# Convolution rows of a two-block layer: statistics copied among the gated tiles, bias and gates loaded in another order, the last row normed in halves

## The reference, cut to what matters

```python
u = h @ w_in + b_in
a, ga, z = split(u, 3)
glu = a * sigmoid(ga)
c = depthwise_conv(glu, w_dw, taps=31) + b_dw
c = silu(layer_norm(c, norm_g, norm_b))
y = (c * silu(z)) @ w_out + b_out
h = layer_norm(DN_ALPHA * h + y, post_ln_g, post_ln_b)   # for each token
```

## Time and profile before

| | |
|---|---|
| runs | 2434.09, 2439.77, 2440.2 us; median 2439.77 |
| profiled execution | 2432.7 us, of it span 2431.0 us |
| PE busy | 2330.9 us, 96% of the span |
| DVE, ACT, POOL busy | 1388.2, 1125.8, 878.7 us |
| convolution's rows | about 535 us to 771 us of the span |

### The profile page before, as it was taken

The page is one execution under the profiler, slowest core; times in us unless marked ns, Lnnn a source line. Parts: engine busy times, 40 slices in busy tenths (PEclk is TensorE's granted clock), DMA queues, the critical chain, the costliest instruction groups (busy, mean ns, idle before and its releaser), DMA issues. The chain is left out here.

```text
span 2431.0 us, 34611 instructions
## 1 busy us (share of the span) xinstructions
PE 2330.9 (96%) x13338; PEld 1214.8 (50%) x13338; DVE 1388.2 (57%) x2330; ACT 1125.8 (46%) x2179; POOL 878.7 (36%) x673
## 2 busy tenths in 40 slices
PE   8999999997997999999999998998899998999998
PEld 4555555543444455555555554444545554444443
DVE  6999999974654234334334334677267776235422
ACT  7766666576653234334344334333155665233311
POOL 3988888877882110101101010443033333000000
PEclk9999999998998999999999999999999999999999
DMA  5011111143333000101000003223410000101322
GB/s 203 29 55 44 37 39 39 47 141 100 126 121 148 1 1 12 46 1 49 1 5 10 1 1 130 79 92 108 64 43 10 19 1 1 40 18 55 110 101 90
DMA packets 52218, 134.67 MB, mean 55 GB/s; under 512 B 5391, under 2 KB 23439, under 8 KB 51032
## 3 DMA queue, kind: packets, MB, share of 16 engines
q1 hardware_dynamic: 52056, 132.46, 16.3%
HBM read 96.65 MB, written 35.80 MB: 54 GB/s over the span
## 5 line engine op out<-in xcount | busy, mean ns | idle before, releaser
L1146 DVE SCALAR_TENSOR_TENSOR cv_tap_sum<-cv_glu,cv_prm,cv_tap_sum 128x1024 f32<-128x1024 f32 x326 | 418.9, 1288 | 11.9 <-ACT cv_tap_sum L648 2.4
L902 POOL TENSOR_TENSOR mixed<-mixed,cv_tap_products 128x1024 f32<-128x1024 f32 x153 | 364.2, 2381 | 77.5 <-ACT cv_tap_products L663 62.1
L91 PE MATMUL cv_proj<-H_hi,cv_w_ga 128*128 128x416 f16 (+1 forms) x640 | 217.0, 339 | 7.9 <-DVE H_lo L1119 7.9
L92 PE MATMUL cv_proj<-H_lo,cv_w_ga 128*128 128x416 f16 (+1 forms) x640 | 217.0, 339 | 0.0
L93 PE MATMUL cv_proj<-H_hi,cv_w_ga 128*128 128x416 f16 (+1 forms) x640 | 217.0, 339 | 0.0
L91 PE MATMUL gm_vr<-gm_wvr_hi,H_hi 128*128 128x512 f16 (+1 forms) x544 | 202.8, 373 | 0.0
L92 PE MATMUL gm_vr<-gm_wvr_lo,H_hi 128*128 128x512 f16 (+1 forms) x544 | 202.8, 373 | 0.0
L93 PE MATMUL gm_vr<-gm_wvr_hi,H_lo 128*128 128x512 f16 (+1 forms) x544 | 202.8, 373 | 0.0
L1769 POOL TENSOR_TENSOR gm_q_inter<-gm_q_rel,gm_block_decays 128x512 f32<-128x512 f32 x16 | 16.8, 1048 | 467.0 <-ACT gm_block_decays L1846 467.0
L663 ACT ACTIVATE cv_tap_products<-cv_glu,cv_prm 128x1024 f32<-128x1024 f32 x138 | 151.8, 1140 | 35.9 <-POOL mixed L902 35.8
L2125 DVE SCALAR_TENSOR_TENSOR gm_v_r<-gm_vr,gm_v_r 128x256 f32<-128x256 f32 x64 | 27.2, 425 | 236.9 <-ACT gm_v_r L1865 236.9
(11 more groups left out here) (443 smaller groups left out, 5751.8 us busy)
## 6 DMA issues: line engine op xcount, KB each, us to landing
cv_w_stage<-conv_w SPq DMA_DIRECT2D x24, 512.0 KB, 3.9
mixed<-gla_w SPq DMA_DIRECT2D x8, 1024.0 KB, 6.7
go_rows<-h_rows SPq DMA_DIRECT2D x16, 512.0 KB, 3.9
h_rows<-go_rows SPq DMA_DIRECT2D x16, 512.0 KB, 2.8
pl_sums_a<-h_rows SPq DMA_DIRECT2D x16, 512.0 KB, 3.5
out<-pl_sums_a SPq DMA_DIRECT2D x16, 512.0 KB, 2.6
cv_tap_products<-gate_z SPq DMA_DIRECT2D x24, 256.0 KB, 3.9
mixed<-xT SPq DMA_DIRECT2D x12, 416.0 KB, 8.0
```

Source lines behind the costliest of these rows:

```text
L91: nc.tensor.matmul(out, w_hi, x_hi, start=first, stop=False)
L92: nc.tensor.matmul(out, w_hi, x_lo, start=False, stop=False)
L902: nc.gpsimd.tensor_tensor(c_unit(U), c_unit(U), prod[:, r % 3, :], ALU.add).then_inc(s_add, 1)
L1146: nc.vector.scalar_tensor_tensor(out=acc_unit(U), in0=window(U, k), scalar=col(U // 2, k), in1=acc_unit(U), op0=ALU.mult, op1=ALU.add).the ...
```

## The change

1. ACT copies the sums of group 2 between the gated tiles 5 and 6 of group 1, before it norms row 0; they were copied after it, at row 1. The tiles themselves keep their order.
2. For groups 3 and 4 (rows 3 and 7), ACT copies the sums before the row's root and norming; it did so after them.
3. SP loads the bias and row 1 before the wait for the last convolution product, and the first gates of group 1 after it; five of these gates now stand ahead of the two layer-norm vectors, three did before. ACT scales the bias before gated tiles 0 and 1 of group 1, and POOL adds it to row 0 before them.
4. The last row is normed by ACT in two halves; DVE copies the low half of row 14 before it multiplies and adds the vectors of the last row, no longer after; and the last row's transposes go to two PSUM banks of its own (those of the means and spreads), so that they wait for no copies of row 15, only for the group statistics to be used up (`c_n`).

```diff
+        last_pt = [acc[:, 512 * h:512 * h + 512] for h in range(2)]
+        def turned(s, h):
+            return (last_pt if s == LAST else pt)[h]
...
                 for b in range(2):
                     sp.wait_ge(s_szo[b], 16 * KT * NTT // 2)
-                sp.wait_ge(s_add, slot(UNITS - 1, n_products(UNITS - 1)) + 1)
-                for k in range(R):
-                    load_gate(1, k)
                 sp.wait_ge(o_lo, KT)
                 vector(bias_bc, bias_dram, s_bv)
                 load_row(1)
+                sp.wait_ge(s_add, slot(UNITS - 1, n_products(UNITS - 1)) + 1)
+                for k in range(R + 2):
+                    load_gate(1, k)
                 sp.wait_ge(c_m, KT)
                 vector(g_bc, g_dram, s_vec)
                 vector(b_bc, b_dram, s_vec)
                 for s in range(NS + 1):
                     if s == 0:
-                        for k in range(R, KT):
+                        for k in range(R + 2, KT):
                             load_gate(1, k)
...
                 squares(2, range(CG))
-                gated(1, range(2))
                 act.wait_ge(s_bv, 16)
                 nc.scalar.activation(bias_bc, bias_bc, ACT.Copy, scale=1.0 / ALPHA).then_inc(s_bias, 1)
+                gated(1, range(2))
                 squares(2, range(CG, KT))
+                gated(1, range(2, 6))
+                copy_sums(2)
+                gated(1, range(6, KT))
                 for s in range(NS + 2):
-                    gated(*UNITS_AT.get(s, (0, ())))
-                    if (s, 0) in SUMS:
-                        copy_sums(SUMS[s, 0])
+                    if s:
+                        gated(*UNITS_AT.get(s, (0, ())))
...
+                    if (s, 1) in SUMS:
+                        copy_sums(SUMS[s, 1])
                     if s < NS:
...
-                        nc.scalar.activation(tile(s), tile(s), ACT.Identity, scale=sd[0:n, b, 1:2],
-                                             bias=sd[0:n, b, 2:3]).then_inc(s_u, 1)
-                    if (s, 1) in SUMS:
-                        copy_sums(SUMS[s, 1])
+                        for h in range(2) if s == LAST else (slice(0, 2),):
+                            x = tile(s).rearrange("p (a n) -> p a n", a=2)[:, h]
+                            mm = nc.scalar.activation(x, x, ACT.Identity, scale=sd[0:n, b, 1:2], bias=sd[0:n, b, 2:3])
+                            mm.then_inc(s_u, 1)
...
+                add_bias(0)
                 gated(1, range(2))
-                add_bias(0)
...
-                        if s:
+                        if s == LAST:
+                            pe.wait_ge(c_n, len(GROUPS) * KT)
+                        elif s:
                             pe.wait_ge(s_th, 2 * s + h - 1)
                             pe.wait_ge(s_tl, 2 * s + h - 1)
```

More of the change, by code:

```diff
@@ L874, in _ @@
                             nc.scalar.activation(H_hi[:, 4 * h:4 * h + 4, at:at + n],
-                                                 pt[h].rearrange("p (k n) -> p k n", k=4)[:, :, 0:n], ACT.Copy).then_inc(s_th, 1)
+                                                 turned(s - 2, h).rearrange("p (k n) -> p k n", k=4)[:, :, 0:n],
+                                                 ACT.Copy).then_inc(s_th, 1)
+                    if (s, 1) in SUMS:
+                        copy_sums(SUMS[s, 1])
                     if s < NS:
@@ L1043, in transposes @@
                             c = (4 * h + q) * P
-                            mm = nc.tensor.transpose(pt[h][:, q * P:q * P + n], tile(s)[:, c:c + P], ident[0:n, 0:n])
+                            mm = nc.tensor.transpose(turned(s, h)[:, q * P:q * P + n], tile(s)[:, c:c + P], ident[0:n, 0:n])
                         mm.then_inc(s_tr, 1)
@@ L1277, in _ @@
                                                 ALU.mult).then_inc(s_nm, 1)
[L1278 to L1285, removed]
                     if s >= 2:
@@ L1290, in _ @@
                             nc.vector.tensor_tensor(H_lo[:, 4 * h:4 * h + 4, at:at + n],
-                                                    pt[h].rearrange("p (k n) -> p k n", k=4)[:, :, 0:n],
+                                                    turned(s - 2, h).rearrange("p (k n) -> p k n", k=4)[:, :, 0:n],
                                                     H_hi[:, 4 * h:4 * h + 4, at:at + n], ALU.subtract).then_inc(s_tl, 1)
+                    if s == LAST:
+                        for h in range(2):
+                            c = slice(h * 512, h * 512 + 512)
+                            dve.wait_ge(s_vec, 16 * 2)
+                            dve.wait_ge(s_u, NS + h)
+                            nc.vector.tensor_tensor(tile(LAST)[:, c], tile(LAST)[:, c], g_bc[:, c], ALU.mult).then_inc(s_lg, 1)
+                            dve.wait_ge(s_lg, h + 1)
+                            nc.vector.tensor_tensor(tile(LAST)[:, c], tile(LAST)[:, c], b_bc[:, c], ALU.add).then_inc(s_lh, 1)
 def gla_out(nc, ahead, next_loads, rows_in, vecs, rows_out, pre_g, gs, M, H_hi, H_lo):
```

## The result

The changed kernel took 2423.26 us in the median of 4 runs, the kernel before 2439.58 us: a ratio of 0.9941, 95% interval 0.9922 to 0.9959. That is 14 us by the ratio (16.3 between the medians) where 8.55 us were forecast. Timed again with 12 runs against 20 of the kernel before, the ratio was 0.9969 (0.9956 to 0.9982), 7.6 us of 2435.6. The profiled executions lie 9.1 us apart, 2432.7 and 2423.57 us.

A forecast was written before the change was run, and what follows sets the result against it. The prediction took POOL, ACT and DVE, releasing one another, to bound the kernel until row 13. It summed 4.2 us there and 4.35 us at the last row to 8.55 us, forecasting 2431.2 us from 2439.77, range 2425 to 2437.

The forecast's parts named there:

- The bound: Until row 13: POOL, ACT and DVE waiting on one another set the pace; PE's earlier gains are waited away there.
- the ring: POOL, ACT and DVE releasing one another tile after tile until row 13; its start, mean_square(2), moves 4.2 us sooner.
- PE's waits: Rival for the rows: PE's waits of 7.4, 2.8 and 0.4 us bound and return; 19 us in all, chance 0.07.
- Copies of group 2: Before row 0's norming: earlier copies let mean_square(2) start at 556.2 us instead of 560.42, gaining 4.2 us.
- POOL's stall: At gate 6 of group 1: POOL waits for a silu issued behind the copies, 1.35 us (bounds 0 and 2.2).
- PE's new idle before row 2: Before row 2: PE waits anew for the low parts of group 1, some 2.5 us.
- Bias and gates: At group 1's first tiles: bias lands 4.25 us after issue, gates in time, and tile 3's 1.11 us gate wait goes.
- The start: Mean_square(2), with earlier copies, bias and gates: everything until row 13 comes 4.2 us sooner.
- Later copies: Groups 3 and 4, copied before the rows' norming: PE's 2.78 and 0.37 us waits go, worth 0.
- The last row: At the end: last DVE instruction and barrier come 4.35 us sooner, bounds 3.5 and 4.9.
- slow behind its gap: Row 15's transposes: PE taken at the 1.2 GHz level after its idle, 1.94 us for eight.
- Sum: Whole kernel: 4.2 us until row 13 plus 4.35 us at the end, 8.55 us.

The follow-up runs named there:

- late_copies_only: Kernel before with only the copies of groups 3 and 4 moved ahead of the rows' norming; ratio 1.0011 (1.0001 to 1.0022).
- start_only: Kernel before with group 2's copies among the gated tiles and the new bias and gate order, no later copies or end; ratio 0.9984 (0.9974 to 0.9994).
- silu_first: Changed kernel with the silu of group 1's tile 6 issued before tile 5's high part and group 2's copies; ratio to the kernel before 0.9968.
- copies2_only: Kernel before with only group 2's copies moved among the gated tiles; row 13 at 175.63 us behind the memset, no ratio given.
- after_again: The changed kernel timed and traced once more, no further edit; ratio to the kernel before 0.9969 (0.9956 to 0.9982).
- after: The changed kernel's first trace, against the kernel before; profiled execution 2423.57 us.
- before_again: The kernel before timed and traced once more as a control, no edit; ratio 1.0004 (0.9993 to 1.0014).
- end_only: Kernel before with only the change's edits of the last row; ratio 0.9989 (0.9977 to 1.0).
- best: Changed kernel with the silu of tile 6 issued earlier, but bias and gate loads and bias order as before; ratio 0.9958 (0.9943 to 0.9974).
- bias_only: Kernel before with only the new order of bias and gates, no moved copies; row 13 at 178.82 us behind the memset, no ratio given.

## Why the prediction came out as it did

**The bound.** Right: the ring of POOL, ACT and DVE sets when row 13 starts, and taking PE's own waits away gains nothing. late_copies_only shows it from one side, start_only from the other (2.8 to 4.1 us where PE's waits promised 7 and more).

**Copies of group 2.** The mechanism and its terms hold: mean_square(2) foreseen at 556.2, measured at 556.43 in an execution 0.4 us late; POOL's stall 1.35 foreseen, 1.33 measured; PE's new idle before row 2 some 2.5 foreseen, 3.17 measured. silu_first shows that the stall was a cost of this order and not of the copies.

**Bias and gates.** The landing was 4.1 us after the issue (4.25 taken), and no gate held the first tiles. The 3.2 us that the prediction works out from the Trainium skill's page "DMA: Bandwidth & Descriptors" are too short for it; the page gives that fit for transfers issued by GpSimd, and these are SyncE's. But I compared with one trace, in which a late gate cost 1.11 us at tile 3; only that trace and copies2_only (0.67 us) show such a wait among the eight with the old loads (with the new ones after_again alone waits, 0.23 us at a later tile). Wrong was to let the early bias count as a gain of the ring. With the old loads ACT and POOL gate tiles 0 and 1 while the bias is on its way; with the new ones they do it after the bias, which takes POOL 3.7 us, and the 4 us of earlier landing only pay for that. With the old loads the ring's start follows the landing: in the five traces without a late gate the square stands 21.8 us behind it (7.64 and 29.46, 9.46 and 31.24). Behind three gates the bias took 6.2 to 8.0 us from its issue in the eight traces, ahead of them 4.1 to 4.5 us in the five with the new loads. So the new loads seem mostly to narrow the spread, row 13 at 175.2 to 175.6 in three traces where the six with old loads and old copies spread over 1.8 us. The start is worth 3.6 us against the mean of the old ones; 4.2 was mis-sized by the late gate.

**Later copies.** 0, as foreseen, and for the reason foreseen (late_copies_only).

**The last row.** 4.35 foreseen, 4.15 measured. That PE was taken to be slow behind its gap was wrong in part: the gap of 2.81 us was not always followed by the slow level. Eight transposes took 1.23 us in `after`, 1.94 in silu_first.

**Sum.** 3.6 + 4.15 = 7.75 us against 8.55; GLA begins 8.1 us sooner than in before_again, of which 0.8 us are the clock's column, and after_again's ratio says 7.6. The first median, 2423.26, lies under the range's 2425 and 8 us under the 2431.2 forecast. What I left out of the range is the scatter of medians of few runs: the base of the forecast, 2439.77 from three runs, was 2435.6 in 20 later ones, and the changed kernel's 2423.26 was 2428.17 in 12. The terms of the sum did not cause the miss; of the 16.3 us between the two first medians about half was chance.

## What to carry to other kernels

Before adding up an engine's waits, look further down for a wait in which it will lose what it wins: the 4.5 us at row 13 told that 3 us of earlier waits were worth nothing. Put small copies that another engine waits for among paced work, but behind the instruction that feeds the pacing engine; here the order of one silu decided over 1.3 us. An operand that arrives sooner gains nothing if work that used to fill the wait for it is put behind it: here that work took the 4 us back.

## What the runs showed of the hardware

**A stall without a releaser.** In 4 of the 13 traces PE stands for 8.8 to 10.7 us, 40 to 46 us into the attention layer, and no semaphore ends the wait. The end of it in after_again's timeline, the window around it (us, busy of PE, PEld, DVE, ACT, POOL, granted clock, DMA share, GB/s), and a row of the DMA queues from 1743.1 to 1744.3 us (packets, MB, share):

```profile
1745.49 0.29 PE L93 MATMUL at_p_probsT<-at_probs,H_lo 128*128 128x128 f16 x1 [10.41 <-issue]
```
```profile
1730.00:1750.00 20.00, 9.59 (x135) 9.42 (x132) 0.69 (x1) 0.60 (x1) 0.00 (x0) 0.69 0.47 50
```
```profile
q8 instruction: 1, 0.02, 4.6%
```

From the first load of attention weights to their last low half it takes 234.5 to 239.5 us in these four and 231.7 to 232.1 in the other nine. It happened with and without the change (late_copies_only, end_only, after_again, best). What the DMA records show is that PE goes on just after an instruction packet of 16 KB has landed: in after_again at 1744.1 us, PE at 1745.5. In all four long stalls, and in three short ones of 1.5 to 1.9 us some 18 us ahead of them, it is 1.4 to 1.6 us behind such a landing. In `after` these packets start at 1724.5 and 1731.6 us, in after_again at 1725.4 and 1743.2, with none between. So PE most likely waited for its own instructions; no run tested it. Why the packet came late stays open: the transfer that keeps the queues 47% busy at 50 GB/s runs in `after` too (0.48 and 51 GB/s from 1720 to 1740 us), and PE doesn't stall there.

**The clock at the end of attention.** What follows that stretch differs by another 3.6 us between traces (439.7 to 443.3). start_only and bias_only, the ends of this range, have the same waits there, and their clocks part behind this one (start_only first):

```profile
2039.50 0.38 PE L91 MATMUL at_p_gate<-H_hi,at_w_hi 128*128 128x512 f16 x1 [2.98 <-DVE at_gate L2563]
```
```profile
2043.78 0.58 PE L91 MATMUL at_p_gate<-H_hi,at_w_hi 128*128 128x512 f16 x1 [2.98 <-DVE at_gate L2561]
```

Behind one and the same idle of 2.98 us PE goes on at the 2.4 GHz level in one trace and at 1.2 GHz in the other; from this matmul to the first of the pooling layer it is 27.83 us at a mean granted clock of 0.84 in start_only and 30.97 us at 0.72 in bias_only. PE is busy 17.05 and 20.22 us of it, and DVE, ACT and POOL are each busy as long in both within 0.1 us, so these 3.1 us are the clock's. Stall and clock together are as large as the change, enough to make medians of few runs mislead.

**The clock after row 13.** From row 13 to the end of row 14's transposes the same work took 46.40 to 48.01 us in 13 traces. Behind the wait the granted clock was 0.83 over the first 12.6 us in `after`, where the first matmul took 0.61 us, the 1.2 GHz level; from 717.8 us on it was 1.00, 2.4 GHz. The Trainium skill's "TensorE: Matmul & The Clock Gate" (section "What you observe") says that the point of the rise varies from run to run. The traces here don't show that at this place: the two kernels that were traced twice repeat within 0.1 us (48.01 and 47.98, 47.15 and 47.06), and the spread of 1.6 us is between kernels.

```profile
705.20:717.80 12.60, 12.60 (x50) 5.42 (x51) 2.27 (x5) 2.20 (x3) 12.44 (x6) 0.83 0.30 109
```
